# Throwaway matmuls, earlier weight rounding, and a gate chain moved into the value units of a four-layer hybrid trunk

## The reference, cut to what matters

```
for layer i in 0..3:
    h = rmsnorm(x, norm_mix_g[i])
    0: x += chunk_mlp(h)           # gMLP spatial gating
    1: x += multiscale_pool(h)     # trailing means over 2/4/8/16 positions minus the token,
                                   # then a 256x256 map per channel group and a scale
    2: x += conformer_conv(h)      # GLU, depthwise conv 31, layernorm, silu, pw2
    3: x += gated_deltanet(h)      # q/k/v with short conv and silu, q and k l2-normalised,
                                   # beta = sigmoid(ab), g = -exp(a_log)*softplus(ab + dt_bias),
                                   # delta rule in chunks of 64, rmsnorm * silu(h @ w_g), out
    h = rmsnorm(x, norm_ffn_g[i])
    x += (silu(dwconv3(h @ w_up_a)) * (h @ w_up_b)) @ w_down
return rmsnorm(x), new states
```

## Time and profile before

| | us |
|---|---|
| median of 3 runs (lowest, highest) | 1626.18 (1625.86, 1628.54) |
| the profiled execution, its own time | 1627.81 |
| its span, first to last instruction | 1626.1 |
| TensorE busy in the span | 1560.9 (96%) |
| VectorE, ScalarE, GpSimd busy | 811.0, 712.8, 1058.5 |
| mean granted TensorE clock | 0.983 |

### The profile page before, as it was taken

The page is one execution under the profiler, slowest core; times in us unless marked ns, Lnnn a source line. Parts: engine busy times, 40 slices in busy tenths (PEclk is TensorE's granted clock), DMA queues, the critical chain, the costliest instruction groups (busy, mean ns, idle before and its releaser), DMA issues.

```text
span 1626.1 us, 32573 instructions
## 1 busy us (share of the span) xinstructions
PE 1560.9 (96%) x10386; PEld 1507.1 (93%) x10386; DVE 811.0 (50%) x1782; ACT 712.8 (44%) x1364; POOL 1058.5 (65%) x994
## 2 busy tenths in 40 slices
PE   5999999999999999998999999899999999999997
PEld 5999999998999998885999999899888888999997
DVE  3355555016555414877555531465667776555402
ACT  5555444444444434224644434546434333544432
POOL 5557887754777678541777767666655556777674
PEclk9999999997999999999999999999999999999999
DMA  5434444542444655220455545544412224444353
GB/s 191 128 113 161 146 146 158 143 114 95 151 153 155 153 149 165 68 78 26 138 165 165 157 120 148 166 130 130 138 37 85 87 89 152 142 154 153 116 153 107
DMA packets 87740, 212.47 MB, mean 131 GB/s; under 512 B 25488, under 2 KB 33200, under 8 KB 87536
## 3 DMA queue, kind: packets, MB, share of 16 engines
q1 hardware_dynamic: 87664, 211.49, 42.4%
HBM read 201.80 MB, written 9.66 MB: 130 GB/s over the span
## 4 chain that ended last, share of the span: by engine, by line
PE 90%; DVE 5%; ACT 2%; issue 1%; DMA 1%; POOL 1%; DVEq 0%; SPq 0%; POOLq 0%; ACTq 0%
PE bank L770 25%; PE bank L771 25%; PE bank L772 25%; PE bank L982 4%; PE bank L1115 1%; PE bank L1137 1%; PE bank L1126 1%; DVE ssq L1740 1%; PE bank L1175 1%; PE bank L1023 1%; ACT Gh L1294 0%; DMA raw<-in_a_in 0%; DMA fst<-in_d_st 0%; PE bank L1205 0%; DVE Gl L1730 0%
## 5 line engine op out<-in xcount | busy, mean ns | idle before, releaser
L574 POOL TENSOR_TENSOR wlo<-raw,whi 128x512 fp32r<-128x512 f32 (+3 forms) x404 | 463.4, 1147 | 422.9 <-ACT whi L1259 389.1
L770 PE MATMUL bank<-Gh,whi 128*128 128x320 f32 x1928 | 605.7, 314 | 23.8 <-DVE Gl L1730 18.6
L771 PE MATMUL bank<-Gl,whi 128*128 128x320 f32 x1928 | 598.0, 310 | 0.0
L772 PE MATMUL bank<-Gh,wlo 128*128 128x320 f32 x1928 | 598.0, 310 | 0.0
L576 POOL TENSOR_TENSOR wlo<-raw,whi 128x512 fp32r<-128x512 f32 (+2 forms) x404 | 480.6, 1190 | 0.0
L1259 ACT ACTIVATE whi<-raw 128x1024 fp32r<-128x1024 f32 (+3 forms) x404 | 375.6, 947 | 53.1 <-PE bank L772 42.8
L770 PEld LDWEIGHTS bank<-Gh,whi 128*128 128x128 f32 x1928 | 363.8, 189 | 28.2 <-issue 18.2
L771 PEld LDWEIGHTS bank<-Gl,whi 128*128 128x128 f32 x1928 | 364.2, 189 | 1.5
L772 PEld LDWEIGHTS bank<-Gh,wlo 128*128 128x128 f32 x1928 | 363.9, 189 | 0.0
L770 PE MATMUL bank<-Hh,whi 128*128 128x320 f32 x912 | 286.8, 314 | 8.3 <-DVE Hl L1723 6.3
L771 PE MATMUL bank<-Hl,whi 128*128 128x320 f32 x912 | 283.8, 311 | 0.0
(11 more groups left out here) (336 smaller groups left out, 1810.5 us busy)
## 6 DMA issues: line engine op xcount, KB each, us to landing
raw<-in_f_up SPq DMA_DIRECT2D x176, 512.0 KB, 3.4
raw<-in_f_down SPq DMA_DIRECT2D x64, 384.0 KB, 3.2
raw<-in_f_down SPq DMA_DIRECT2D x64, 320.0 KB, 3.2
raw<-in_c_pw SPq DMA_DIRECT2D x24, 512.0 KB, 3.6
raw<-in_a_in SPq DMA_DIRECT2D x16, 512.0 KB, 3.6
raw<-in_d_qk SPq DMA_DIRECT2D x16, 512.0 KB, 4.1
raw<-in_d_vg SPq DMA_DIRECT2D x16, 512.0 KB, 3.6
raw<-in_a_out SPq DMA_DIRECT2D x8, 512.0 KB, 3.5
```

What stands on the lines that cost most here:

```text
L574: pool.tensor_tensor(wlo[k][:, 0:half], raw[k][:, 0:half], whi[k][:, 0:half].bitcast(F32), ALU.subtract).then_inc(half_ready, 1)
L770: nc.tensor.matmul(dst, wh, h, start=start and n == 0, stop=False)
L771: nc.tensor.matmul(dst, wh, lo, start=False, stop=False)
L772: ins = nc.tensor.matmul(dst, wl, h, start=False, stop=stop and end and n == len(tiles) - 1)
```

## The change

1. A helper `fill(n)` issues n products of 128 x 320 from a tile of Hh into PSUM bank 0; nobody reads them. It is called with 8 after the turn of X tile 6 and with 8 after the row norms in the pooling layer, and with 32 in front of c_pw2.
2. In the pooling layer ScalarE rounds the weights two tiles further ahead: units 2 and 3 before the tile loop, unit m + 4 in tile m; the wait for the pooling state stands in tile 0 behind them. VectorE's reciprocal covers only the last 79 of 320 columns, those that are read.
3. The gate chain moves from the q/k units to the value units. Exp and Ln stand behind value pair 1, gT and Sigmoid behind pair 3, Sqrt behind pair 4, Exp behind pair 5, the copy of the columns behind pair 6. TensorE's turn of G1 stands after value unit 5, the cumulative sum after unit 7, both further turns after unit 11. VectorE's parts stand behind pairs 2, 4, 5, 6 and 7. The order of the semaphore counts is changed to fit.
4. SyncE stores the rows after it has issued the last four value loads, not before.

```
         G_READY, RW_READY, RN_READY, ROWS_READY = 3, 4, 5, 6
-        GT_READY, RW_READY_A = 5, 7
+        LN_READY, GT_READY, SQRT_READY, RW_READY_A, COLS_READY = 3, 4, 7, 9, 10
         PAIR_STEPS = 16
...
                             load(name, l, b, k)
-                    gdn_stores()
                     for k in range(SLOTS):
                         load(name, l, 3, k)
+                    gdn_stores()
                     load("d_out", l, 0, 0)
...
+            def fill(n):
+                h = tile_of(Hh, FT - 1)
+                for _ in range(n):
+                    nc.tensor.matmul(acc[0][:, 0:NT], h[:, 0:P], h, start=True, stop=True)
             def column_sums():
...
                 turn_x(KT - 2)
+                pe.wait_ge(evac, START["b_grp", 1] - 4)
+                fill(8)
                 column_sums()
...
                 norm_stat(2)
+                fill(8)
                 u0 = START["b_grp", 1]
...
                     ins.then_inc(csq_read, 1)
+                pe.wait_ge(z_ready, KT)
+                fill(32)
                 out_phase("c_pw2", 2, lambda m: range(KT))
...
                         l2_sum(0, 0)
-                for k in range(4):
-                    in_unit(u0 + 4 + k, k)
-                    l2_sum(k + 1, (k + 1) % 2)
-                    if k == 0:
+                with pe.Fori(1, 4) as b:
+                    for k in range(4):
+                        in_unit(b * 4 + (u0 + k), k)
+                        l2_sum(b * 4 + (k - 3), (k + 1) % 2)
+                u0 = START["d_vg", 3]
+                for k in range(16):
+                    in_unit(u0 + k, k % 4)
+                    if k < 3:
+                        l2_sum(13 + k, (k + 1) % 2)
+                    if k == 5:
                         pe.wait_ge(consts, ZEROS)
...
                         turn(mixb[2], G1).then_inc(ab_t, 1)
-                    if k == 2:
+                    if k == 7:
                         pe.wait_ge(ab_a, GT_READY)
...
                         ins.then_inc(ab_t, 1)
-                with pe.Fori(2, 4) as b:
-                    for k in range(4):
-                        in_unit(b * 4 + (u0 + k), k)
-                        l2_sum(b * 4 + (k - 3), (k + 1) % 2)
-                u0 = START["d_vg", 3]
-                for k in range(8):
-                    in_unit(u0 + k, k % 4)
-                    if k < 3:
-                        l2_sum(13 + k, (k + 1) % 2)
-                    if k == 3:
+                    if k == 11:
                         pe.wait_ge(ab_v, RW_READY)
...
                         turn(mixb[2], RW).then_inc(ab_t, 1)
-                    if k == 6:
                         pe.wait_ge(ab_v, RN_READY)
                         turn(mixb[0], rnc, w=16).then_inc(ab_t, 1)
-                with pe.Fori(2, 4) as b:
-                    for k in range(4):
-                        in_unit(b * 4 + (u0 + k), k)
+                pe.wait_ge(ab_v, ROWS_READY)
+                pe.wait_ge(ab_a, COLS_READY)
                 for i in range(1, 6):
...
                 pe.wait_ge(qk_ready, 24)
-                pe.wait_ge(ab_v, ROWS_READY)
-                pe.wait_ge(ab_a, 10)
...
                 pooled_hi(1)
-                act.wait_ge(pool_state, 2)
+                ahead(u0, 0, 0, 0)
+                ahead(u0, 0, 1, 0)
                 for m in range(KT):
...
                         pooled_hi(m + 2)
-                    ahead(u0, 0, m, 0)
+                    if m + 2 < KT:
+                        ahead(u0, 0, m + 2, 0)
+                    if m == 0:
+                        act.wait_ge(pool_state, 2)
                     residual(3, m, m % 2, evac, u0 + m + 1)
...
                 qk_history(1, 1, 1)
-                act.wait_ge(consts, ZEROS)
-                act.wait_ge(ab_v, 1)
-                nc.scalar.activation(RW[0:32, 0:NT], AB[0:32, 0:NT], ACT.Sigmoid).then_inc(ab_a, 1)
-                act.wait_ge(ab_v, 2)
-                nc.scalar.activation(KD[:, 0:NT], KD[:, 0:NT], ACT.Exp, scale=-1.0).then_inc(ab_a, 1)
-                nc.scalar.activation(dc[:, 0:1], col("d_al"), ACT.Exp).then_inc(ab_a, 1)
-                act.wait_ge(ab_a, 2)
-                nc.scalar.activation(KD[:, 0:NT], KD[:, 0:NT], ACT.Ln, bias=ones[:, 0:1]).then_inc(ab_a, 1)
                 qk_body(0, True)
-                act.wait_ge(ab_t, 1)
-                nc.scalar.activation(gT, mixb[2][:, 0:TW], ACT.Copy).then_inc(ab_a, 1)
                 with act.Fori(1, 3) as b:
...
                 vg_half(0, 0)
+                act.wait_ge(ab_v, 2)
+                nc.scalar.activation(KD[:, 0:NT], KD[:, 0:NT], ACT.Exp, scale=-1.0).then_inc(ab_a, 1)
+                nc.scalar.activation(dc[:, 0:1], col("d_al"), ACT.Exp).then_inc(ab_a, 1)
+                act.wait_ge(ab_a, 1)
+                nc.scalar.activation(KD[:, 0:NT], KD[:, 0:NT], ACT.Ln, bias=ones[:, 0:1]).then_inc(ab_a, 1)
+                vg_half(0, 1)
+                vg_half(1, 0)
+                act.wait_ge(ab_t, 1)
+                nc.scalar.activation(gT, mixb[2][:, 0:TW], ACT.Copy).then_inc(ab_a, 1)
+                act.wait_ge(consts, ZEROS)
+                act.wait_ge(ab_v, 1)
+                nc.scalar.activation(RW[0:32, 0:NT], AB[0:32, 0:NT], ACT.Sigmoid).then_inc(ab_a, 1)
+                vg_half(1, 1)
+                act.wait_ge(l2sums, 16)
+                ns = mixb[0][:, 0:48].rearrange("p (c two) -> p c two", two=2)
+                rs = rnc.rearrange("p (c two) -> p c two", two=2)
+                nc.scalar.activation(rs[:, :, 0], ns[:, :, 0], ACT.Sqrt, scale=float(P), bias=dc[:, 1:2]).then_inc(ab_a, 1)
+                nc.scalar.activation(rs[:, :, 1], ns[:, :, 1], ACT.Sqrt, bias=eps[:, 0:1]).then_inc(ab_a, 1)
+                vg_half(2, 0)
                 act.wait_ge(ab_v, RW_READY)
...
                 nc.scalar.activation(RW[KDEC:KDEC + 32, 0:NT], KD[KDEC:KDEC + 32, 0:NT], ACT.Exp).then_inc(ab_a, 1)
-                vg_half(0, 1)
-                act.wait_ge(l2sums, 16)
-                ns = mixb[0][:, 0:48].rearrange("p (c two) -> p c two", two=2)
-                rs = rnc.rearrange("p (c two) -> p c two", two=2)
-                nc.scalar.activation(rs[:, :, 0], ns[:, :, 0], ACT.Sqrt, scale=float(P), bias=dc[:, 1:2]).then_inc(ab_a, 1)
-                nc.scalar.activation(rs[:, :, 1], ns[:, :, 1], ACT.Sqrt, bias=eps[:, 0:1]).then_inc(ab_a, 1)
-                vg_half(1, 0)
+                vg_half(2, 1)
                 act.wait_ge(ab_t, 3)
...
                                      ACT.Copy).then_inc(ab_a, 1)
-                vg_half(1, 1)
-                with act.Fori(2, 3) as b:
-                    vg_half(b, 0)
-                    vg_half(b, 1)
                 vg_half(3, 0)
...
                 dve.wait_ge(std_ready, 3)
-                vec.reciprocal(R[:, :], sd[:, :]).then_inc(r_ready, 1)
+                vec.reciprocal(R[:, SEQ - 15:NT], sd[:, SEQ - 15:NT]).then_inc(r_ready, 1)
                 h0, u0 = htile(1, False), START["b_grp", 1]
...
-                qk_body(0, (0, 1))
-                dve.wait_ge(ab_a, 4)
+                qk_body(0)
+                with dve.Fori(1, 4) as b:
+                    S.enter(b, 1, 4 * 4)
+                    qk_body(b)
+                S.leave(1, 3)
+                def vg_half(b, x):
+                    uv, h = b * 4 + (START["d_vg", 3] + 2 * x), b * 2 + x
+                    qk_front(uv, b * 2 + (16 + x), 2 * x, x, b * 6 + (3 * x + 2))
+                    dve.wait_ge(unit_done, uv + 2)
+                    vec.tensor_tensor(tile_of(GT, h), acc[2 * x + 1][:, 0:NT], R[:, :], ALU.mult).then_inc(evac, 1)
+                vg_half(0, 0)
+                vg_half(0, 1)
+                dve.wait_ge(ab_a, LN_READY)
                 S.mark(vec.scalar_tensor_tensor(out=KD[:, 0:NT], in0=XG[:, 0:NT], scalar=0.0, in1=KD[:, 0:NT],
...
                 vec.tensor_scalar(G1[:, 0:NT], KD[:, 0:NT], dc[:, 0:1], -1.0, ALU.mult, ALU.mult).then_inc(ab_v, 1)
-                qk_body(0, (2, 3))
-                qk_body(1)
+                vg_half(1, 0)
+                vg_half(1, 1)
                 dve.wait_ge(ab_t, 2)
...
                 vec.tensor_copy(RW[GC:GC + 32, 0:NT], G1[GC:GC + 32, 0:NT]).then_inc(ab_v, 1)
-                with dve.Fori(2, 4) as b:
-                    S.enter(b, 2, 4 * 4)
-                    qk_body(b)
-                S.leave(2, 2)
-                def vg_half(b, x):
-                    uv, h = b * 4 + (START["d_vg", 3] + 2 * x), b * 2 + x
-                    qk_front(uv, b * 2 + (16 + x), 2 * x, x, b * 6 + (3 * x + 2))
-                    dve.wait_ge(unit_done, uv + 2)
-                    vec.tensor_tensor(tile_of(GT, h), acc[2 * x + 1][:, 0:NT], R[:, :], ALU.mult).then_inc(evac, 1)
-                vg_half(0, 0)
-                vg_half(0, 1)
-                dve.wait_ge(ab_a, 9)
+                vg_half(2, 0)
+                dve.wait_ge(ab_a, SQRT_READY)
                 vec.reciprocal(rnc, rnc).then_inc(ab_v, 1)
-                vg_half(1, 0)
```

(25 more changed lines are left out.)

3 lines of the change are left out of this document (removed).

## The result

The change makes the kernel faster, by about half of what was forecast. After it takes 1618.5 us (median of 8 runs, 1614.3 to 1619.4) against 1626.9 us before (8 runs, 1622.4 to 1630.6): ratio 0.9947, 95% interval 0.9930 to 0.9964. Run once more beside other kernels it was 1619.1 against 1627.3 us, ratio 0.9954 (0.9935 to 0.9973). Forecast were 1610.0 us and a gain of 16.2 us; measured are 8.4 and 8.2 us, outside the range of 1606 to 1617 us. The profiled execution after took 1618.48 us, its span is 1616.8 us, 9.3 us less than before.

The account below looks back on a forecast made before the run. TensorE, busy for 96% of the span, was taken as the bound. Pooling 9.9 + gate chain 6.3 + LayerNorm 0 + value units 0 = 16.2 us, from a median of 1626.18 to 1610.0 us; range 1606 to 1617.

Parts of the forecast that it names:

- it waits for the unit that X also waits for and ends before Gh can start, so it is free: Pooling: ScalarE's rounding two tiles ahead, 0.41 us per b_grp unit, was claimed to cost nothing.
- that contention as a term: Pooling: GpSimd's f_up lo halves beside VectorE's operations, put at 2.66 us, bounds 0 and 5.2.
- 9.9: Pooling: gain in us, last group of the first f_up unit at 391.5 instead of 401.4; bounds 7.3 to 12.5.
- The clock then stays at 2.4 GHz: Pooling: with two batches of 8 products TensorE works 4.1 of 4.7 us and keeps full clock.
- rival A: Pooling: the clock falls all the same; gain 2.3 + 6.3 = 8.6 us, 1617.6 us; chance 0.10.
- The LayerNorm: Conformer layer, 32 products ahead of c_pw2: put at 0, ends +1.7 (clock falls later, a unit half at 1.2 GHz) and -1.0.
- The gate chain, 6.3 us: DeltaNet q/k units: gain from moving the chain out, 3.6 us plus 2.7 us of half clock; 5 to 7.
- Silu at +0.1 us and no half clock: First q unit: sign of being right, Silu some 0.1 us behind its convolution and no half clock there.
- The value units: DeltaNet: the moved gate chain costs 0 there, ends -1 and +5; TensorE without a gap.
- B: Value units: the first long insertion reaches TensorE by its whole 5.1 us; 1615.1 us; chance 0.08.
- C: Value units starve: each insertion reaches TensorE and brings half clock; 10.1 us slower, 1636.3 us; chance 0.04.
- D: Whole kernel: rival A, and the chain's 6.3 us come back at the end; within 0.2%, about 1624; chance 0.04.

Follow-up runs that it names:

- e11: e7 plus 12 throwaway products in TensorE's stop in c_pw1, in front of the second GLU pair; 1613.1 us, ratio 0.9923.
- e5: After with the pooling roundings in their old order and without the 32 products ahead of c_pw2; 1614.2 us, ratio 0.9937.
- e2: After with the pooling layer's roundings back in their old order; 1616.8 us, ratio 0.9943.
- e6: e2 plus four throwaway products before each further tile of c_pw2's first unit, batch of 32 kept; 1614.4 us, ratio 0.9937.
- e7: e5 plus the DeltaNet's convolution history loaded ahead of its masks, on its own semaphore; 1613.5 us, ratio 0.9930.
- e12: e7 run again unchanged, beside after on the same chip; 1613.6 us, ratio 0.9913.
- e8: After with the pooling layer's roundings one tile ahead instead of two; 1614.7 us, ratio 0.9935.
- e4: After without the two batches of 8 throwaway products in pooling; 1621.9 us, ratio 0.9984.
- e1: After without the 32 throwaway products ahead of c_pw2; 1617.8 us, ratio 0.9953.
- e9: After run again unchanged, beside other kernels on one chip; 1619.1 us, ratio 0.9954.
- e10: e5 with the reciprocal over all 320 columns again; 1618.6 us, ratio 0.9942.
- e3: Before with only the gate chain moved: no throwaway products, roundings in old order, wide reciprocal; 1621.9 us, ratio 0.9973.

## Why the prediction was wrong

**The step that failed, in pooling: "it waits for the unit that X also waits for and ends before Gh can start, so it is free".** I costed the rounding on ScalarE alone, where that is so (VectorE waited 0.68 us for the first Gh, and 0.63 before). What it sets off is on GpSimd: there the lo halves are queued behind the states, so that four units' roundings were ready when the states were done, and eight halves ran without a break over VectorE's first Gl. I had that contention as a term (2.66 us, up to 5.2), but only for the f_up halves later on. These came as well. The pile cost 2.8 us of VectorE, then the stop of 1.28 us in TensorE, and with it 6.8 us at half clock. So pooling gained 5.5 us instead of 9.9 in the profile of after, and 4.6 in the second (6.0 in the stage, 1.4 lost right behind it). Shown: with the batches and the narrow reciprocal, the first Gl takes 3.33 us two tiles ahead, 2.50 one ahead and 0.55 none ahead. The stage takes 31.43 to 32.95 us two tiles ahead, 30.69 one ahead (32.1 with the fall just behind it), 29.02 to 29.18 none ahead, and once 30.39 (e11); the part that the clock adds differs from execution to execution. With the old order the forecast's other steps hold within 0.5 us (9.4 gained in e5), but in e2, e6, e7 and e12 the clock fell once more, over dense conv units, and took 1.5 us of it back.

The Trainium skill (SBUF — State Buffer, on who interferes with whom) let one side hold the port for a whole instruction, and I took 1.3 us as the price of one lock. Here VectorE stood for eight instructions of the other engine in a row, not one; e8 shows the same with six. For the 128x512 halves of f_up one lock each is right, since VectorE came in between them (387.17 above). The long hold was seen only with the 128x128 halves, which follow each other every 0.42 us; why it is so there is not shown.

**The clock.** "The clock then stays at 2.4 GHz" held from 360 to 376 and, with the old order, through all pooling tiles; rival A (it falls anyway, gain 2.3 in pooling) is what e4 without the batches looks like, with 1.6 us. In after, e1 and e9 it fell behind a stop that the change itself made, and not in the seven profiles with the batches and the narrow reciprocal where no stop of more than 0.44 us stands there.

**The LayerNorm, put at 0 with a cost of 1.7 us as one end: it cost 2.0 us in the profile, 1.0 in the second.** The mechanism of that end was written down (the clock falls later, and a unit runs at 1.2 GHz), and I gave it no weight. Before, the fall lay under work that VectorE paces and cost nothing; there was nothing to win and something to lose.

**The gate chain, 6.3 us: 4.5 in the profile of after, 5.6 in the second, 6.0 in six others (5.9 in e10; 3.5 in e2, where the clock fell once more and the history was late), 6.7 with the history first.** Silu at +0.1 us and no half clock were right. The convolution's start was not VectorE's to give: its first operation of the layer, from which the convolution follows, already waited for the history load before. ScalarE's copy, which waits for it too, started at 1043.63 and VectorE 0.52 us later, as in every profile with the masks first:
```profile
1043.63 0.34 ACT L1525 ACTIVATE fpad<-fst 128x24 f32<-128x24 f32 x2 [1.50 <-DMA fst<-in_d_st]
```
I took the start of the convolution as given, and nothing of that load's lateness was in the sum. In after's profile it cost 1.4 us. The value units were right: no gap, so rivals B and C are refuted. D is refuted by the ratio. (TensorE would have been free at 1054.52 - 3.52 = 1051.0, not 1050.9, which changes nothing.)

**The sum, in the two profiles:** start 0.3, pooling 5.5, c_pw2 -2.0, DeltaNet 4.5, heads 1.0, together 9.3 us. Against 16.2 that is 4.4 less in pooling, 2.0 in c_pw2, 1.8 in DeltaNet, and 1.3 more from start and heads, which the forecast did not have. The medians give 8.4 us; the heads' 1.0 lies within their spread, last section, and the execution profiled before was 0.9 us above the median of the 8 runs.

## What to carry to other kernels

Where work is moved ahead on one engine, follow it through every queue behind: what was spread out may arrive in one lump, and a lump of short GpSimd operations held VectorE for its whole length here (3.33 us for eight), where longer ones held it one at a time. Throwaway products are worth their place where dense work follows the gap at once (the pooling batches, 3.9 us between e4 and after, 2.6 between e3 and e10); in front of a unit that another engine paces they only move the fall of the clock onto the dense work behind it. And ask of every stage that gets shorter which load comes next: here it was 288 KB queued behind 772 KB that nobody needed yet.

## What the runs showed of the hardware

The heads ran 214.5 to 220.0 us in the thirteen profiles with the gate chain moved, with the same instructions. Windows of after, then of e3, whose heads began 0.3 us apart:
```profile
1236.00:1240.00 4.00, 4.00 (x24) 4.00 (x23) 2.58 (x7) 3.02 (x7) 3.68 (x3) 0.57 0.00 0
1240.00:1250.00 10.00, 10.00 (x73) 8.51 (x73) 6.07 (x14) 2.99 (x5) 7.12 (x5) 1.00 0.01 4
```
```profile
1236.00:1240.00 4.00, 4.00 (x28) 4.00 (x28) 3.28 (x8) 3.97 (x10) 4.00 (x5) 0.72 0.00 0
1240.00:1250.00 10.00, 10.00 (x57) 10.00 (x58) 2.64 (x10) 0.40 (x2) 3.56 (x3) 0.60 0.00 0
```
After has 3.4 us at half clock there and e3 has 10.2, and in ten us of full TensorE work 73 matmuls stand against 57. Where thin TensorE work brings the clock down, the fall doesn't come at the same instruction in each execution; on paced work it costs nothing, on dense work it costs somewhat under half its length (1.5 us for 3.4 in conv and in DeltaNet). That this makes most of the difference between executions fits the granted clock of those without a profile: of the 35 executions of before in the comparison with e1, the fastest (1621.3 us) had a mean clock of 0.988 and the slowest (1635.0 us) 0.977, and by and large the times between them rise as the clock falls. In which stage it fell there is not recorded. For this kernel a difference under 2 us is seen in the stages of a profile and not in the medians.
